# Context decay sums of a gated linear attention layer computed from rounded parts, with the first decay step placed earlier

## What is computed

```python
def gla_log_decay(lowrank, w_gk, b_gk):
    g = jax.nn.log_sigmoid(lowrank @ w_gk + b_gk) / GLA_GATE_NORM          # 16
    return gla_heads(g, GLA_DK)                                            # 4 heads of 128

def gla_final_state(k, v, g):
    b = jnp.cumsum(g, axis=2)                                              # over 256 tokens
    return jnp.einsum('bhtd,bhte->bhde', k * jnp.exp(b[:, :, -1:] - b), v)

s_f = gla_final_state(kgc, vgc, gfc)
s_b = gla_final_state(flip_t(kgc), flip_t(vgc), flip_t(gbc))
mod_x = jnp.split(jax.nn.silu(c) @ w_ada[l] + b_ada[l], 6, axis=-1)        # rows of modulation
```

## Time and profile before

| | |
|---|---|
| Time, median of 3 runs | 881.21 us (880.62 to 882.29) |
| The profiled execution | 880.8 us |
| Its span | 878.9 us |
| PE busy | 864.6 us, 98% of the span |
| DVE busy | 641.1 us, 73% |
| ACT busy | 495.5 us, 56% |
| POOL busy | 22.2 us, 3% |
| Granted PE clock | 0.998 of full speed (2.4 GHz) |

### The profile page before, as it was taken

One profiled execution on the slowest core, in us unless ns is written; L12 is line 12 of the kernel. 1 busy time (PEld: TensorE's weight loads), 2 busy tenths in 40 slices (PEclk: granted clock), 3 DMA queues, 4 the chain that ended last, 5 costly groups with the idle time before them and its releaser, 6 DMA issues.

```text
span 878.9 us, 14252 instructions
## 1 busy us (share of the span) xinstructions
PE 864.6 (98%) x5122; PEld 730.7 (83%) x5122; DVE 641.1 (73%) x1014; ACT 495.5 (56%) x802; POOL 22.2 (3%) x36
## 2 busy tenths in 40 slices
PE   8999999999999999999999999999999999999996
PEld 6888888887788888888888888988889888888885
DVE  3579898888879978876555568767777855555575
ACT  4586787756575665474444444453755544444554
POOL 0010000000011200100000000000000000000001
PEclk9999999999999999999999999999999999999999
DMA  9953434235447786636555557354434865555531
GB/s 362 371 152 125 129 109 143 97 120 192 144 167 261 235 289 224 225 124 213 192 191 186 194 188 272 102 191 134 144 126 139 280 245 185 192 191 189 173 123 49
DMA packets 45267, 161.90 MB, mean 184 GB/s; under 512 B 5501, under 2 KB 5661, under 8 KB 45217
## 3 DMA queue, kind: packets, MB, share of 16 engines
q1 hardware_dynamic: 43200, 156.78, 52.6%
q0 software_dynamic: 1296, 3.78, 1.6%
q10 hardware_dynamic: 720, 0.65, 0.2%
HBM read 160.15 MB, written 1.05 MB: 183 GB/s over the span
## 4 chain that ended last, share of the span: by engine, by line
PE 69%; DVE 16%; ACT 6%; issue 4%; DMA 4%; POOL 0%; SPq 0%; POOLq 0%; DVEq 0%; ACTq 0%
PE bank L817 41%; PE bank L1194 12%; PE bank L1199 6%; DVE w_lo L1946 4%; DVE small L1976 3%; DMA arena<-in_early 2%; DMA raw<-in_stream 2%; PE bank L1015 1%; ACT w_hi L1427 1%; DVE arena L2332 1%; PE bank L1005 1%; ACT gx_more L1659 1%; PE bank L1321 1%; PE bank L963 1%; PE bank L1022 1%
## 5 line engine op out<-in xcount | busy, mean ns | idle before, releaser
L817 PE MATMUL bank<-w_hi,act 128*128 128x512 f32 (+1 forms) x1456 | 453.3, 393 | 0.3 <-DVE w_lo L1946 0.2
L1946 DVE TENSOR_TENSOR w_lo<-raw,w_hi 128x1024 fp32r<-128x1024 f32 x244 | 287.9, 1219 | 56.9 <-ACT w_hi L1427 56.1
L817 PEld LDWEIGHTS bank<-w_hi,act 128*128 128x128 f32 x1456 | 267.1, 188 | 53.5 <-issue 1.6
L817 PE MATMUL bank<-w_lo,act 128*128 128x512 f32 (+1 forms) x728 | 282.4, 388 | 0.0
L1427 ACT ACTIVATE w_hi<-raw 128x1024 fp32r<-128x1024 f32 x244 | 245.6, 1051 | 64.9 <-PE bank L817 42.1
L817 PEld LDWEIGHTS bank<-w_lo,act 128*128 128x128 f32 x728 | 136.7, 188 | 28.7
L1194 PE MATMUL bank<-act,w_hi 128*128 128x512 f32 x448 | 111.8, 391 | 0.0
L1194 PEld LDWEIGHTS bank<-act,w_hi 128*128 128x128 f32 x448 | 81.3, 189 | 15.1
L1427 ACT ACTIVATE act<-arena 128x512 fp32r<-128x512 f32 (+1 forms) x65 | 39.5, 630 | 63.7 <-DVE arena L2404 33.0
L817 PE MATMUL bank<-act,w_hi 128*128 128x256 f32 x384 | 71.7, 287 | 1.1 <-DVE act L1946 0.7
L2390 DVE TENSOR_TENSOR arena<-bank,arena 128x512 f32<-128x512 f32 x28 | 19.2, 690 | 64.0 <-ACT arena L1746 64.0
(11 more groups left out here) (282 smaller groups left out, 762.0 us busy)
## 6 DMA issues: line engine op xcount, KB each, us to landing
raw<-in_stream SPq DMA_DIRECT2D x278, 512.0 KB, 4.4
arena<-in_early SPq DMA_DIRECT2D x16, 512.0 KB, 11.5
res<-in_x SPq DMA_DIRECT2D x2, 512.0 KB, 4.4
arena<-in_ctx SPq DMA_DIRECT2D x2, 512.0 KB, 10.8
res<-in_x POOLq DMA_DIRECT2D x1, 1024.0 KB, 7.1
arena<-in_norm_final POOLq DMA_DIRECT2D x1, 512.0 KB, 4.6
arena<-in_ple_b POOLq DMA_DIRECT2D x1, 512.0 KB, 5.3
out<-arena ACTq DMA_DIRECT2D x2, 256.0 KB, 2.7
```

The lines of the kernel that those rows point to most:

```text
L817: last = pe.matmul(o, left, right, start=start and m == 0, stop=stop and m == 2, skip_group_check=shared)
L1946: return dve.tensor_tensor(o, x, hi.bitcast(F32), ALU.subtract)
```

## The change

1. **Parts of the decays.** Behind `gs_g` ACT now rounds `gs_a` to `gs_hi` (`gla_context_hi`) and DVE subtracts to get `gs_lo`, both at the end of `("gstate", h)`, for all four heads. PE's sums wait for `gs_lo` and take, for each direction, four fp32r matmuls: the triangle by the high and by the low part, both token halves at once (256 columns), and ones by the high and by the low part of the other half (128 columns).
2. **The first decay step.** `("gstate", 0)` moves from behind the key step `k[1]` to ahead of it.
3. **Modulation row 10** is no longer split: one full float32 matmul with 512 columns takes the place of two fp32r ones, and POOL's cut of it is gone.
4. **Rounded triangles and ones.** POOL rounds both triangles (256 columns) and the ones (128 columns) once, when the last level product of the GLA is done; before, it rounded the ones after attention. `gs_hi` and `gs_lo` share the space of the row parts.

```diff
-    p.woven("aq0", lv[c:] + [("gsfirst",), k[0], k[1]])
     gs = [("gstate", j) for j in range(6)]
-    p.woven("aq1", [gs[0], k[2], gs[1], k[3], gs[2], k[4], gs[3], q[0]])
+    p.woven("aq0", lv[c:] + [("gsfirst",), k[0], gs[0], k[1]])
+    p.woven("aq1", [k[2], None, gs[1], k[3], gs[2], k[4], gs[3], q[0]])
...
+            pool.wait_ge(lv_mm, len(BATCHES) * GH)
+            pool.wait_ge(params_in, 16 * N_PARAMS)
+            pool.tensor_copy(later_r[:, 2 * NC:2 * NC + 2 * P], consts[:, 1:3, :].rearrange("p m n -> p (m n)")).then_inc(pool_done, 1)
+            pool.tensor_copy(ones_r, ones).then_inc(pool_done, 1)
...
-            pool.wait_ge(res_ready, RES_AT["n2"] + 2)
-            fin_cut(10)
...
-                if tile == GT_TILES[-1]:
-                    pe.wait_ge(ada_sum_done, ADA_ORDER.index(tile) + 1)
-                    return pe.matmul(o[:, :], ones, ada_sum, start=True, stop=True)
-                pe.wait_ge(fin_cut_done, 2 * GT_TILES.index(tile) + 3)
-                pe.matmul(o[:, :], ones_r, fin_lo, start=True, stop=False)
-                return pe.matmul(o[:, :], ones_r, fin_hi, start=False, stop=True)
+                if tile in SPLIT_TILES:
+                    pe.wait_ge(pool_done, ROOT_SET + 2 * SPLIT_TILES.index(tile) + 2)
+                    pe.matmul(o[:, :], ones_r, fin_lo, start=True, stop=False)
+                    return pe.matmul(o[:, :], ones_r, fin_hi, start=False, stop=True)
+                pe.wait_ge(ada_sum_done, ADA_ORDER.index(tile) + 1)
+                return pe.matmul(o[:, :], ones, ada_sum, start=True, stop=True)
...
-                    pe.wait_ge(gs_g, h + 1)
+                    pe.wait_ge(gs_lo_done, h + 1)
                     if h >= 1:
                         pe.wait_ge(gs_exp, h)
-
-                    for d, tri, summed in ((0, l_strict, 0), (1, u_strict, 1)):
-                        for t in range(2):
-                            o = psum[5][:, (2 * t + d) * P:(2 * t + d + 1) * P]
-                            last = pe.matmul(o, tri, gs_a[:, t, d, :], start=True, stop=(t != summed))
-                            if t == summed:
-                                last = pe.matmul(o, ones, gs_a[:, 1 - t, d, :], start=False, stop=True)
+                    else:
+                        pe.wait_ge(pool_done, TRI_SET)
+                    sums = psum[5][:, :].rearrange("p (t d n) -> p t d n", t=2, d=2)
+                    for d, tri, summed in ((0, l_strict_r, 0), (1, u_strict_r, 1)):
+                        pe.matmul(sums[:, :, d], tri, gs_hi[:, :, d], start=True, stop=False, skip_group_check=True)
+                        pe.matmul(sums[:, :, d], tri, gs_lo[:, :, d], start=False, stop=False, skip_group_check=True)
+                        pe.matmul(sums[:, summed, d], ones_r, gs_hi[:, 1 - summed, d], start=False, stop=False,
+                                  skip_group_check=True)
+                        last = pe.matmul(sums[:, summed, d], ones_r, gs_lo[:, 1 - summed, d], start=False, stop=True,
+                                         skip_group_check=True)
...
+                if h < GH:
+                    gla_context_hi(h)
...
+            def gla_context_hi(h):
+
+                act.wait_ge(gs_g, h + 1)
+                hi_part(gs_hi, gs_a).then_inc(gs_hi_done, 1)
...
                     dve.scalar_tensor_tensor(out=flat, in0=psum[4][:, :], scalar=0.0, in1=flat, op0=ALU.min,
                                              op1=ALU.subtract).then_inc(gs_g, 1)
+                    dve.wait_ge(gs_hi_done, h + 1)
+                    lo_part(gs_lo, gs_a, gs_hi).then_inc(gs_lo_done, 1)
```

More of the change, by code:

```diff
@@ L61 @@
 GT_TILES = (4, 5, 10, 11)
+SPLIT_TILES = (4, 5)
 def mlp_tiles(tag):
@@ L391 @@
 ROOT_ON_POOL = ("n2",)
-ZEROS_SET, PICKS_SET, ROOT_SET = 1, 3, 4
+ZEROS_SET, PICKS_SET, TRI_SET, ROOT_SET = 1, 3, 5, 6
 SCALED_LATER = ("n3", "n4", "n5")
@@ L445, in build @@
         gx_c = sb("gx_c", [P, 2, 2, 32])
-        with nc.sbuf_tensor("fin_r", [P, 2 * NC + P], F32R) as fin_r:
-            fin_hi, fin_lo, ones_r = fin_r[:, 0:NC], fin_r[:, NC:2 * NC], fin_r[:, 2 * NC:2 * NC + P]
+        with nc.sbuf_tensor("later_r", [P, 2 * NC + 3 * P], F32R) as later_r:
+            gs_hi, gs_lo = (later_r[:, i * NC:(i + 1) * NC].rearrange("p (t d n) -> p t d n", t=2, d=2) for i in range(2))
+            u_strict_r, l_strict_r, ones_r = (later_r[:, 2 * NC + i * P:2 * NC + (i + 1) * P] for i in range(3))
+            fin_hi, fin_lo = later_r[:, 0:NC], later_r[:, NC:2 * NC]
         gx_more = sb("gx_more", [P, N_LVL - 3, 2 * T])
@@ L604, in build @@
         ada_sum_done = sem("ada_sum_done")
-        fin_cut_done = sem("fin_cut_done")
         gain_ready = sem("gain_ready")
@@ L617, in build @@
         go_sig, gomul_done, sig_ready = sem("go_sig"), sem("gomul_done"), sem("sig_ready")
-        gs_mm, gs_ln, gs_g, gs_cum, gs_exp, gs_kd, gs_out, gs_copy = (
-            sem(n) for n in ("gs_mm", "gs_ln", "gs_g", "gs_cum", "gs_exp", "gs_kd", "gs_out", "gs_copy"))
+        gs_mm, gs_ln, gs_g, gs_hi_done, gs_lo_done, gs_cum, gs_exp, gs_kd, gs_out, gs_copy = (
+            sem(n) for n in ("gs_mm", "gs_ln", "gs_g", "gs_hi_done", "gs_lo_done", "gs_cum", "gs_exp", "gs_kd", "gs_out",
+                             "gs_copy"))
         gx_mm, gx_ln, gx_g, gx_scan, gx_eq, gx_qin = (
@@ L758, in _ @@
             pool.memset(pick_r[:, :].bitcast(F32), 0.0).then_inc(pool_done, 1)
[L759 to L765, removed]
             wait_cut(pool, UNIT["gk", 3])
@@ L780, in _ @@
                 pool.dma_start(b_rows[32 * r:32 * r + 1, :], a["b_rows"][r:r + 1, :]).then_inc(b_rows_in, 16)
[L781 to L784, removed]
+            for i, tile in enumerate(SPLIT_TILES):
+                pool.wait_ge(ada_sum_done, ADA_ORDER.index(tile) + 1)
+                pool.tensor_copy(fin_hi, ada_sum).then_inc(pool_done, 1)
+                pool.wait_ge(pool_done, ROOT_SET + 2 * i + 1)
+                pool.tensor_tensor(fin_lo, ada_sum, fin_hi.bitcast(F32), ALU.subtract).then_inc(pool_done, 1)
             pool.wait_ge(gout_done, GH)
```

## The result

The changed kernel takes **883.79 us** (median of 10 runs, 881.74 to 886.18) against 881.40 (10 runs, 880.62 to 882.61): ratio 1.0027 [1.0019, 1.0036], 2.4 us slower. The forecast of 882.6 is 1.2 too low, inside its range; it was called "the same within 0.2%" and is slower by a little more. Five of the ten executions have a granted clock of 0.995 and take 884.29 to 886.18 us, the other five 0.996 to 0.998 and 881.74 to 883.30. The profiled execution took 883.3 us (before 880.8), its span is 881.5 (before 878.9).

The account below looks back on a forecast made before the run. PE and DVE were taken as nearly level bounds of the state stretch. 1.2 (states) + 0 (row 10) + 0.2 (POOL) = +1.4 us, 880.8 to 882.2 profiled; forecast median 882.6 us, range 879.8 to 884.6.

Parts of the forecast that it names:

- The walk through the heads: Context states, 150 to 211 us: head-by-head waits of DVE and PE; both engines leave the stretch 0.9 us late.
- The shift handed on from 211 us: Value product of attention waiting for DVE at 210.95: moves by 1.0 to 1.2 us; +1.2 us taken.
- The narrow fp32r matmul: 128-column ones matmuls in PE's decay sums: taken at 0.11 us each, bounded by 0.06 and 0.22.
- Rival 1: PE's decay sums: narrow fp32r matmuls cost what full ones do, 0.22 us, so PE saves nothing; 883.6 us, chance 0.32.
- rival 3: DVE-ACT round trips and PE's new waits: hand-overs take 0.1 us instead of 0.05; 883.4 us, chance 0.10.
- Rival 2: State stretch: DVE's new waits fall into its idle times, PE's saving of 1.7 to 2.5 passes; 879.1 us, chance 0.12.
- Row 10: Unsplit modulation sum: 0.4 us more PE time falls into a 0.47 us gap waiting for DVE; effect nothing.
- POOL's roundings: Ones and triangles rounded ahead of the state stretch beside DVE work: collisions cost 0 to 1.7 us, +0.2 taken.
- The row that priced a collision: Profile row before the change: DVE's subtraction beside POOL's took 2.09 us instead of 1.22; a collision costs up to 0.87.
- The sum: Whole kernel: 1.2 for the states, 0 for row 10, 0.2 for POOL's roundings, +1.4 us in all.
- The term that failed: Behind the value product at 210.95: PE, busy almost throughout, passes the +1.2 us shift on to the end.

Follow-up runs that it names:

- filled_mid: Changed kernel with the first decay step right behind key step k[1] and each low part made behind other DVE work; ratio 0.9996 to the kernel before.
- moved_only: Kernel before with only the first decay step moved ahead of the key step k[1]; ratio 1.0010 to the kernel before.
- delay_half: Kernel before plus three full float32 matmuls of 128 columns on PE (0.67 us) at the end of state step 3; ratio 1.0012 to the kernel before.
- parts_moved: Changed kernel with modulation row 10 still split and cut on POOL; ratio 1.0022 to the kernel before.
- delay_only: Kernel before plus six full float32 matmuls of 128 columns on PE (1.33 us) at the end of state step 3; ratio 1.0028 to the kernel before.
- filled_old: Changed kernel with the first decay step in its old place and each low part behind other DVE work; ratio 1.0009 to the kernel before.
- parts_unmoved: Changed kernel with the first decay step in its old place and row 10 split, leaving only the sums from parts; ratio 1.0016 to the kernel before.
- row10: Kernel before with only modulation row 10 unsplit and its POOL cut gone; ratio 0.9997 to the kernel before.

## Why the prediction was right, and where it was short

**The walk through the heads** holds step by step. DVE's keys' products were to start at 162.9, 168.8, 174.2 and 180.3; they start at 163.09, 169.05, 174.37 and 180.72. PE's state products were to start at 163.7, 169.6, 176.7 and 182.1; they start at 163.83, 169.82, 177.16 and 182.55. The waits were put at 0.5 (logarithm), 0.7 (rounding) and 0.6 (guess) and measured 0.44, 0.70 and 0.58. The shift handed on from 211 us is 1.34 us where 1.2 was taken. What was short is head 2. PE starts the state product of head 1 at 169.82, 0.22 us later than the walk has it, and then the sums of head 2, which follow it, have to wait for the low part: their second matmul comes 172.01 - 169.82 = 2.19 us behind the state product, in the last head 179.00 - 177.16 = 1.84. That is 0.35 us lost (the waits above have 0.4), where the walk had 0.2. And a head's sums saved 0.38 and not 0.43. So the walk ended 0.9 us late where the profile has 1.29 on PE and 1.34 on DVE; the forecast's 1.2 is near them because the prediction went from 0.9 to 1.0 to 1.2 and took the upper end, and it shows no row for that: in so far it is luck.

**The narrow fp32r matmul.** Taken at 0.11 us between 0.06 and 0.22; a pair takes 0.07 + 0.11 = 0.18, so 0.09 each. **Rival 1 is out.** The 81 ns of the Trainium skill, TensorE: Matmul & The Clock Gate, "Back-to-back issue gap", is close to this row. The slow weight path for float32 (the Trainium skill, same page, "Weight-path perf modes") doesn't show as a bound above 0.09 us here. The matmuls with 256 columns took 0.12, and 0.12 and 0.17 in the second direction (158.04 and on).

The total alone would have misled: 883.79 is nearest to the 883.6 of rival 1 and the 883.4 of rival 3, both of which the rows rule out.

**Rival 2**, the trips hide, fell where the text said it would: in head 0 DVE had no idle time. That it is the order and not the work which costs, filled_mid shows. **Rival 3** is out: hand-overs of 0.03 to 0.04 us.

**Row 10** at nothing: right, by a run of its own.

**POOL's roundings**, +0.2: wrong, it is 0. The timelines of POOL and DVE at that place:

```profile
144.62 0.40 POOL L773 CAST later_r<-consts 128x256 fp32r<-128x256 f32 x1 [96.97 <-PE bank L1112]
144.97 0.29 POOL L774 CAST later_r<-consts 128x128 fp32r<-128x128 f32 x1
```

```profile
144.59 0.23 DVE L2324 COPY_PREDICATED gx_c<-lvl_mask,bank 128x64 f32<-128x64 uint8 x1 [0.80 <-PE bank L1112]
145.25 1.23 DVE L1954 TENSOR_TENSOR w_lo<-raw,w_hi 128x1024 fp32r<-128x1024 f32 x1 [0.42 <-ACT w_hi L1428]
```

They end as DVE starts its next long instruction, and the only DVE instruction beside them takes 0.23 us, as it did before them. Nothing that could be slowed lies there. The row that priced a collision overlapped POOL's for 360.41 - 359.42 = 0.99 us and lost 0.87, a little less than the full hold that the prediction called it. The hold of a two-input vector instruction by one of GpSimd (the Trainium skill, SBUF — State Buffer, "SBUF: two separate sides") has no place to act here, and no run here tests it.

**The sum** was +1.4 with the 0.2 that isn't there; by the profile's states and by the lowest times it is +1.2 to +1.3 (1.1 for the lowest). **The term that failed** is "behind it PE is busy almost throughout and passes the shift on", with nothing added: the medians differ by 2.4 us. The profiled execution has a longer wait for the stream's loads at 327 us, and the pairs that were made for it say that this is not a fixed price of being late. It comes and goes: 1.2 and 1.0 in the profiles of moved_only and delay_half, none in those of parts_moved and delay_only, whose medians are up by nearly as much as the changed kernel's.

The granted clock of each execution separates a part of the medians. The changed kernel's five executions at 0.995 have a median of 884.90 us, the five at 0.996 to 0.998 one of 882.76, which is 1.4 above before, as the states are. By an estimate, 0.003 of the clock over 883 us is worth 2.6 us to an engine that is busy for 98% of the span; the two medians are 2.1 apart. In parts_moved five of eleven executions have 0.996 (median 883.28, the other six 882.60). None of the 109 executions of the other eleven kernels, and none of the 87 of the kernel before in their sets, is below 0.997. The changed kernel and parts_moved are also the only ones in whose profile PE, between its first 12 us and its last matmul, stands for over 2 us in one place (2.13 and 2.14 at head 0; the longest elsewhere are 1.32 in filled_old and 1.23 in parts_unmoved). That this stand brings the lower clock is not shown: in both profiles the clock is 1.00 (2.4 GHz) from 160 to 170 us, and no execution below 0.997 was profiled.

The clock doesn't explain delay_only, whose ten executions all have 0.997 or 0.998 and whose median is 2.5 up. Why the medians of some kernels lie 1.0 to 1.7 us above their lowest times at that clock and those of others 0.2 to 0.6, I can't say. The sets ran on different chips, and within one set (row10 and delay_only, 0.3 and 1.6) it differs too. What stays open is thus how the changed kernel's last 1.1 us divides between the lower clock and the place where its loads fall, and what lowers the clock; the price of the state stretch is the 1.3.

## What to carry to other kernels

When an operand is split into parts between two engines, put the rounding where the rounding engine is free, and put other work of the subtracting engine between its request and its subtraction. A gain on the busiest engine of a stretch is worth only as much as the engine next to it has room in the very place where it gets the new work: 5.4 us of idle time in the stretch did not hold 5.2 us of new work, since at the first head there was none. For differences of 1 us in a kernel that waits for loads anywhere, compare the lowest of some ten runs, the shift of fixed instructions in the timeline and the granted clock of each run beside the medians.

## What the hardware showed that was not expected

- A pair of fp32r matmuls with 128 columns and their own weights takes 0.18 us from start to start, a full float32 one of the same width 0.22 by itself.
- The same delay of 2.67 us on PE costs 2.3 us by the medians and 2.7 by the lowest times, one of 1.33 us in the same place 2.5 and 1.4. Medians of ten executions of this kernel can't tell one from the other.
- The profiled executions of the thirteen changed kernels differ by -0.5 to +1.3 us in how long the stretch between 325 and 376 us takes, at a granted clock of 0.997 to 0.998; row10, with nothing changed ahead of that stretch, has +0.3.
- Eleven of the 21 executions of the two kernels in which PE stands for 2.1 us in one place have a granted clock of 0.995 or 0.996, and none of 196 others is below 0.997. An execution of the changed kernel at 0.995 takes about 2.1 us more than one at 0.996 to 0.998.
